# Hymba-style block on one core: the output projection moved into a stage of its own, as Strassen blocks per pair of token tiles

## What is computed

```python
h = rmsnorm(x, norm1_w);  proj = h @ w_in            # 1024 -> 2816
qa, ka, va, qb, fb, ib, gb = split(proj)
ya = sliding_window_attention(qa, ka, va, ...)       # 512 columns, 8 heads, window of 2 chunks of 64
yb = hgrn2(qb, fb, ib, gb, ...)                      # 512 columns, 4 heads, gated linear recurrence
x = x + concat(ya, yb) @ w_out                       # 1024 -> 1024: the output projection
h = rmsnorm(x, norm2_w);  gate, up = split(h @ w_gate_up)
x = x + (silu(gate) * up) @ w_down                   # d_ff = 2816
```

## Time and profile before

| | us |
|---|---|
| median of 3 runs | 2197.1 (2196.92 to 2197.79) |
| the profiled execution's own time | 2197.5 |
| its span, first to last instruction | 2195.7 |
| phase A, until the last matmul of WO3 | 894.85 |
| output projection in blocks 0 to 3, from its first matmul to the next block's | 51.86, 51.81, 51.85, 48.87 |

### The profile page before, as it was taken

The page is one execution under the profiler, slowest core; times in us unless marked ns, Lnnn a source line. Parts: engine busy times, 40 slices in busy tenths (PEclk is TensorE's granted clock), DMA queues, the critical chain, the costliest instruction groups (busy, mean ns, idle before and its releaser), DMA issues.

```text
span 2195.7 us, 30926 instructions
## 1 busy us (share of the span) xinstructions
PE 2139.9 (97%) x12376; PEld 1856.1 (85%) x12376; DVE 1337.5 (61%) x1967; ACT 904.7 (41%) x1575; POOL 132.6 (6%) x138
## 2 busy tenths in 40 slices
PE   7999999999999998799999999999999999999999
PEld 7889988998899888788888888888888888888887
DVE  4675367636753677567777667777777764444432
ACT  4774377437733762433323334333233332222221
POOL 2101110120012000100000000000000000000000
PEclk9999999999999999899999999999999999999999
DMA  3322232223223326634445335554444575645532
GB/s 138 136 78 91 102 136 78 97 97 139 75 97 105 136 82 237 229 117 141 156 152 187 101 115 187 177 191 140 164 155 146 181 253 175 214 166 179 186 132 91
DMA packets 156271, 316.22 MB, mean 144 GB/s; under 512 B 9504, under 2 KB 96800, under 8 KB 140128
## 3 DMA queue, kind: packets, MB, share of 16 engines
q1 hardware_dynamic: 144864, 265.74, 35.5%
q0 software_dynamic: 11264, 48.50, 6.1%
HBM read 230.85 MB, written 83.36 MB: 143 GB/s over the span
## 4 chain that ended last, share of the span: by engine, by line
PE 58%; DMA 0%; issue 0%; DVE 0%; POOLq 0%
PE b_bank_A L248 4%; PE b_bank_A L249 4%; PE b_bank_A L250 4%; PE b_bank_B L249 4%; PE b_bank_C L249 4%; PE b_bank_B L248 4%; PE b_bank_C L248 4%; PE b_bank_C L250 4%; PE b_bank_B L250 4%; PE b_hx_bank L1614 3%; PE b_hx_bank L1615 3%; PE b_hx_bank L1613 3%; PE b_bank_D L248 2%; PE b_bank_D L249 2%; PE b_bank_D L250 2%; PE b_hx_bank L1558 1%
## 5 line engine op out<-in xcount | busy, mean ns | idle before, releaser
L248 PE MATMUL a_pj<-a_w_hi,a_hT_hi 128*128 128x256 f32 x896 | 259.5, 290 | 1.7 <-issue 1.7
L249 PE MATMUL a_pj<-a_w_lo,a_hT_hi 128*128 128x256 f32 x896 | 253.6, 283 | 0.0
L250 PE MATMUL a_pj<-a_w_hi,a_hT_lo 128*128 128x256 f32 x896 | 253.6, 283 | 0.0
L1501 ACT ACTIVATE b_s_hi<-b_s_stage 128x1408 fp32r<-128x1408 f32 x56 | 77.4, 1382 | 300.1 <-PE b_hx_bank L1615 149.8
L924 DVE TENSOR_TENSOR a_w_lo<-a_w_stage,a_w_hi 128x2048 fp32r<-128x2048 f32 (+1 forms) x64 | 137.9, 2155 | 72.8 <-ACT a_w_hi L587 72.8
L248 PEld LDWEIGHTS a_pj<-a_w_hi,a_hT_hi 128*128 128x128 f32 x896 | 171.9, 192 | 6.7 <-issue 4.4
L249 PEld LDWEIGHTS a_pj<-a_w_lo,a_hT_hi 128*128 128x128 f32 x896 | 172.0, 192 | 0.0
L250 PEld LDWEIGHTS a_pj<-a_w_hi,a_hT_lo 128*128 128x128 f32 x896 | 171.8, 192 | 0.0
L248 PE MATMUL b_bank_A<-b_h_hi_B,b_w_hi 128*128 128x512 f32 x352 | 137.6, 391 | 0.0
L248 PE MATMUL b_bank_B<-b_h_hi_T,b_w_hi 128*128 128x512 f32 x352 | 137.3, 390 | 0.0
L250 PE MATMUL b_bank_A<-b_h_hi_B,b_w_lo 128*128 128x512 f32 x352 | 137.2, 390 | 0.0
(11 more groups left out here) (280 smaller groups left out, 5526.9 us busy)
## 6 DMA issues: line engine op xcount, KB each, us to landing
a_w_stage<-w_whole SPq DMA_DIRECT2D x56, 1024.0 KB, 4.8
b_gu_stage<-w_gu SPq DMA_DIRECT2D x44, 1024.0 KB, 5.1
b_s_stage<-a_sums SPq DMA_DIRECT2D x56, 704.0 KB, 4.2
a_sums<-b_a SPq DMA_DIRECT2D x88, 256.0 KB, 5.5
a_sums<-b_gate SPq DMA_DIRECT2D x66, 256.0 KB, 4.1
b_hx<-hc POOLq DMA_DIRECT2D x13, 1024.0 KB, 5.3
b_w_blocks<-w_dn SPq DMA_DIRECT2D x11, 1024.0 KB, 4.7
a_x_res<-x_pad POOLq DMA_DIRECT2D x16, 512.0 KB, 5.4
```

Source lines behind the costliest of these rows:

```text
L248: pe.matmul(out, stationary[0](k), moving[0](k), start=(k == 0 and not adds), stop=False, skip_group_check=adds)
L249: pe.matmul(out, stationary[0](k), moving[1](k), start=False, stop=False, skip_group_check=adds)
L250: last = pe.matmul(out, stationary[1](k), moving[0](k), start=False, stop=(k == ends), skip_group_check=adds)
L1501: act.activation(f.s_hi[n % 2][:], f.s_stage[n % 2][:], ACT.Copy).then_inc(f.s_hi_ready, 1)
```

## The change

The chunks WO0 to WO3 leave the blocks. The outputs of attention and recurrence are written to DRAM (`y_parts`) in full precision, without a split. In block 0, POOL works out the sums T1 to T4 of w_out's four blocks of 512 x 512 and they are stored (`wo_sums` in DRAM). Behind the last block stands a stage of its own. It takes token tiles in eight pairs (tile q of one block with tile q of the next): each pair is a 2 x 2 block product by Strassen's scheme in Winograd's form, seven products of 12 matmuls with 512 moving columns in place of eight. The seven right-hand operands (high and low) stay in SBUF, four of them prepared within block 3. The left-hand operands are loaded from `y_parts`; POOL makes the sums S1 to S4, ACT the high and DVE the low parts. DVE adds each product into the residual, which SP loads; ACT squares, SP stores x_mid, and for the pairs 0 to 3 DVE mixes straight from that tile (`scale`, `mix`) in place of the reload in block 3.

The core of the diff:

```diff
-NW = len(CHUNKS) + D // WC
+NW = len(CHUNKS)
...
-    after("I23", 3, ("hb", 3),)
-    after("G23", 0, ("ds", 2, 0), ("ds", 2, 1), ("hc", 3), ("n1a",))
-    after("G23", 1, ("o", 2), ("on1", 2), ("kt", 3), ("n1b", 0), ("n1b", 1))
-    after("G23", 2, ("on2", 2), ("ds", 3, 0), ("ds", 3, 1), ("att", 3))
-    after("G23", 3, ("on3", 2), ("o", 3), ("on1", 3), ("yt", 2), ("n1b", 2), ("on2", 3), ("on3", 3), ("n1b", 3))
-    after("Q23", 1, ("mix", 0, 0))
...
-    after("WO0", 0, ("xT", 0))
...
+    after("I23", 3, ("hb", 3), ("n1a",))
+    after("G23", 0, ("ds", 2, 0), ("ds", 2, 1), ("hc", 3), ("n1b", 0), ("n1b", 1))
+    after("G23", 1, ("o", 2), ("on1", 2), ("kt", 3), ("n1b", 2), ("n1b", 3))
+    after("G23", 2, ("on2", 2), ("ds", 3, 0), ("ds", 3, 1), ("att", 3), ("xT", 0), ("xT", 1))
+    after("G23", 3, ("on3", 2), ("xT", 2), ("xT", 3), ("o", 3), ("on1", 3), ("yt", 2), ("xT", 4), ("xT", 5), ("xT", 6), ("xT", 7))
...
+LAST_HEAD = {("KV", 0): (("on2", HG - 1), ("on3", HG - 1)), ("KV", 1): (("yt", HG - 1),)}
+PRODUCTS_OUT = ("P1", "P5", "P6", "P3", "P7", "P2", "P4")
...
+    at[("KV", 0)] = at.get(("KV", 0), ()) + (("wo_load", 0),)
+    at[("KV", 1)] = at.get(("KV", 1), ()) + (("wo_sums", 0),)
+    at[("KV", 3)] = (("wo_store", 0), ("wo_load", 1))
+    at[("QA0", 0)] = (("wo_sums", 1),)
+    at[("QA0", 2)] = (("wo_store", 1), ("wo_load", 2))
+    at[("QA0", 3)] = (("wo_sums", 2),)
...
+            ("G23", 0): tuple((part, 0, j) for j in (1, 2) for part in ("a_hi", "a_lo")),
+            ("G23", 1): (("t_hi", 3), ("t_lo", 3)),
+            ("G23", 2): tuple((part, 0, j) for j in (3, 4) for part in ("a_hi", "a_lo")),
+            ("G23", 3): tuple((part, 0, j) for j in (5, 6) for part in ("a_hi", "a_lo")) + (
+                ("x_load", 0, 0), ("t_load", 4), ("x_load", 0, 1), ("t_load", 5), ("t_load", 6))}
...
+    after(0, 0, ("on2", HG - 1), ("on3", HG - 1))
+    after(0, 1, ("yt", HG - 1), ("t_hi", 4), ("t_lo", 4), ("a_load", 1))
+    after(0, 2, ("n2w_load",), ("t_hi", 5), ("t_lo", 5))
+    after(0, 3, ("a_sums", 1))
+    after(0, 4, ("t_hi", 6), ("t_lo", 6))
+    for p in range(1, OUT_PAIRS):
+        after(p, 0, *([("a_load", p + 1)] if p + 1 < OUT_PAIRS else []))
+        if p - 1 < MIXED_PAIRS:
+            after(p, 1, ("scale", p - 1))
+            after(p, 2, ("mix", p - 1), ("mix_store", p - 1))
+        if p + 1 < OUT_PAIRS:
+            after(p, 3, ("a_sums", p + 1))
+    for p in range(OUT_PAIRS):
+        if p + 1 < OUT_PAIRS:
+            after(p, 4, *operands(p + 1, 0, 1))
+            after(p, 5, ("x_load", p + 1, 0), *operands(p + 1, 2, 3, 4))
+            after(p, 6, ("x_load", p + 1, 1), *operands(p + 1, 5, 6))
+        after(p, 6, ("mid", p))
...
+        def later_x(b, k):
+
+            if k == KT // 2:
+                for late in (KT - 2, KT - 1):
+                    at = TR_USES.index((b - 1, ("xT", late)))
+                    bank_read(at)
+                    transpose_x(b - 1, late, at, tr[at % 2])
...
+                elif kind == "out":
+                    p, j = step[1:]
+                    name, adds = PRODUCTS_OUT[j], PRODUCTS_OUT[j] in ("P6", "P7", "P3")
+                    pe.wait_ge(a_ready, NPO * p + j + 1)
+                    if p == 0:
+                        pe.wait_ge(t_ready, j + 1)
+                    if j >= 2:
+                        pe.wait_ge(c_added, sums_out(p, j - 1))
```

More of the change, by code:

```diff
@@ L58, in chunk_name @@
 def chunk_name(n):
[L59 removed]
+    return CHUNKS[n][0]
 def chunk_groups(n):
@@ new lines, in out_prepared @@
+def out_prepared():
+    return {("Q01", 0): (("t_load", 0),), ("Q01", 1): (("t_load", 1),),
+            ("I01", 1): (("t_hi", 0), ("t_lo", 0)), ("G01", 0): (("t_hi", 1), ("t_lo", 1)),
+            ("F23", 1): (("t_load", 2),), ("Q23", 1): (("t_hi", 2), ("t_lo", 2)),
+            ("I23", 0): (("a_load", 0),), ("I23", 2): (("a_sums", 0),), ("I23", 3): (("t_load", 3), ("a_hi", 0, 0), ("a_lo", 0, 0)),
+            ("G23", 0): tuple((part, 0, j) for j in (1, 2) for part in ("a_hi", "a_lo")),
[3 more added lines that the diff above has]
+                ("x_load", 0, 0), ("t_load", 4), ("x_load", 0, 1), ("t_load", 5), ("t_load", 6))}
@@ new lines, in out_steps, with after, operands @@
+def out_steps():
+    at = {}
+    def after(p, j, *steps):
+        at.setdefault((p, j), []).extend(steps)
+    def operands(p, *js):
+        return [(part, p, j) for j in js for part in ("a_hi", "a_lo")]
+    after(0, 0, ("on2", HG - 1), ("on3", HG - 1))
[16 more added lines that the diff above has]
+        after(p, 6, ("mid", p))
+    steps = []
+    for p in range(OUT_PAIRS):
+        for j in range(NPO):
+            steps.append(("out", p, j))
+            steps += at.pop((p, j), [])
+    assert not at, at
+    return steps
@@ new lines, in plan @@
+def plan():
+    steps = []
+    for b in range(NB):
+        extra = out_weight_sums({}) if b == 0 else out_prepared() if b == NB - 1 else {}
+        for step in STEPS:
+            if b == NB - 1 and of_next_block(step):
+                continue
+            steps.append((b, step))
+            if step[0] == "proj":
+                place = (chunk_name(step[1]), step[2])
+                if b > 0:
+                    steps += [(b - 1, late) for late in LAST_HEAD.get(place, ())]
+                steps += [(b, early) for early in extra.get(place, ())]
+    return steps + [(NB - 1, step) for step in out_steps()]
@@ L326, in build_phase_a @@
     carry = put("a_carry", [P, HG, P], F32)
+    y_at = mem.at
+    yA = [put(f"a_yA{s}", [P, HG, P], F32) for s in range(2)]
+    yH = [put(f"a_yH{s}", [P, TB], F32) for s in range(2)]
     y_nat = put("a_y_nat", [P, TT, P], F32)
@@ L972, in _ @@
         dve.tensor_scalar(one_less_lb[:], lb[:], -1.0, 1.0, ALU.mult, ALU.add)
-        for b in range(NB):
-            use = 0
-            for step in STEPS:
-                if left_out(step, b):
-                    continue
+        use = 0
+        for b, step in PLAN:
+            if True:
                 kind = step[0]
@@ L1832, in laid_out @@
         "w_whole": np.stack(whole),
+        "w_o": np.stack([rows.reshape(2, KT // 2, P, 2, 512)[k, :, :, half] for k, half in ((1, 1), (0, 1), (0, 0), (1, 0))], axis=2),
         "ident": np.eye(P, dtype=np.float32),
```

647 lines of the change are left out of this document (393 added, 254 removed).

## The result

| | before | after |
|---|---|---|
| median, us | 2197.27 (2196.92 to 2197.79, 4 runs) | 2229.56 (2227.94 to 2230.92, 4 runs) |
| span of the profiled execution | 2195.7 | 2227.5 |

The ratio is 1.0146, 95% interval 1.0134 to 1.0158. The forecast was 2175.3, in a range of 2153 to 2191: the sign was wrong, by 54 us. The part that was predicted to leave PE did leave it; waits in block 0, at the seams, in block 3 and in the new stage, and a lower clock behind most of them, more than made up for it.

The account below looks back on a forecast made before the run. PE, busy 97% of the span, was taken as the bound. Terms -41.5 - 1 + 14.4 - 3.7 + 2 + 3 + 6 - 1 = -21.8 us took the profiled 2197.5 to 2175.7, median 2175.3; range 2153 to 2191.

Parts of the forecast that it names:

- price of a pair, 19.05: Output projection stage: seven products of 12 matmuls take 19.05 us, as one phase B unit; eight pairs 152.4 us.
- block 0: First block: POOL's weight sums delay the powers of the norms behind them, so PE waits; +2 us.
- seams: Three passages between blocks: transposes of the next block wait for DVE's state chain and bank emptying; +14.4 us.
- block 3: Last block: the mixing stall goes, -8.8 us, but operand splits delay the state chain, +5.1; together -3.7 us.
- start of the stage: Beginning of the new output projection stage: 5 MB of loads issued after G23,3 arrive late; +3 us.
- within pairs 1 to 4: Mixing pairs: POOL's sums may hold up DVE, 11 us if so, 0 if not; half taken, +6 us.
- step to phase B: From the last pair to phase B: an earlier end of the stage against 4.5 MB loading at once; -1 us.
- PE's own -41.5: Output projection on PE: 193.9 us of work leaves, 152.4 us comes in; -41.5 us.
- the -1 of small waits: DVE beside PE's work: small waits removed as splits and low parts change; -1 us.
- Rival 2: Pairs 1 to 4: POOL and DVE lock each other, 11 to 16 us, 2180 to 2186; chance 0.20 shared with rival 4.
- Rival 4: Seams: the granted clock falls, 1 to 2 us each, +5, giving 2181; chance 0.20 shared with rival 2.
- Rival 3: Stage pairs: operands come late, each of 7 pairs waits 4 to 5 us, +32, 2198 to 2210; chance 0.09.

Follow-up runs that it names:

- the version without stalls: Changed kernel with block 0, mixture-split, block 3 and seam edits plus three small placement edits, without earlier phase B loads: 2178.8 us, ratio 0.9914.
- where block 3 had been mended: Changed kernel with block 3's preparations each placed where nothing waits behind them, pair 1's operand load not moved: 2214.6 us, ratio 1.0068.
- the three small edits: Pair 1's operands loaded one product earlier, fourth weight tile converted behind G23's last product, two of pair 0's operands within pair 0; not timed alone.
- the last two runs: Changed kernel with all edits together, with and then without the earlier loads of phase B: 2174.7 us (0.9894) and 2178.8 us (0.9914).

## Why the prediction was wrong

By its own steps, with what each term came to in the changed kernel and in the version without stalls (the last of the runs):

| term | predicted | changed | without stalls |
|---|---|---|---|
| price of a pair, 19.05 | 0 | +3.3 | +3.3 |
| block 0 | +2 | +10.8 | +1.2 |
| seams | +14.4 | +20.6 | +14.2 |
| block 3 | -3.7 | +16.6 | -8.5 |
| start of the stage | +3 | +4.1 | +5.5 |
| within pairs 1 to 4 | +6 | +17.7 | +5.9 |
| step to phase B | -1 | +1.2 | +0.9 |

PE's own -41.5 and the -1 of small waits stand beside these terms in the prediction; what was measured of the small waits is in the other rows. In the last column block 0 and block 3 are taken to and from the transposes of k. The seams' 14.2 is 521.83 us for three blocks, less the 653.03 of before without the 145.4 that left; it holds 1.9 us that POOL's moved sums cost in the rest of block 0. Where exactly the last product ends makes some 0.5 us in the sums.

- **PE's work: right, slightly mis-sized.** A pair without mixing takes 19.46 to 19.49 us, not 19.05: 0.4 x 8 = 3.3. The share that the prediction gave to the better price per column, some 11 us, was a slip: its own 169.7 less 152.4 is 17.3. The sum did not use it.
- **Block 3 is the step that failed most.** "That puts the chain 3.6 us later ... together PE reaches the stage 5.1 us late" came out as a wait of 9.72 us with its half clock, and block 3 as 16.6 us longer than before. I followed the state chain of G23,0 but not what came ahead: POOL's sums could only begin at 708.64, behind the split of G23, so the high part came at 714.35, with head 3's decay, its exponentials, a table load and then the next high parts strung behind it. And I had costed `t_lo` 0 and 1 at nothing beside the softmax, where they made waits of 2.87 and 3.63. The last run, with each step in a harmless place, shows that the work itself costs block 3 next to nothing: it then takes 8.5 us less than before, as "-8.8" said, while the stage's start, where two operands went, costs 1.4 more.
- **Within the pairs: mechanism named, wrong half taken.** The prediction gave 11 us "if DVE were held up alike" and took 6. It was held up: 17.7 us, in the pairs 2 to 4 2.6 to 2.7 us of waiting each plus the clock's 1.7. "The trace shows POOL held up, never DVE" is a right reading of the trace before, in which DVE's two-input operations run beside a power unhindered (53.16 above). But a power of 10 columns is not a sum of 512, and the trace before had no such sum; I let the one stand for the other. Rival 2's mechanism is the true one; its size lacked the clock.
- **The granted clock: dismissed wrongly.** Rival 4 was argued away with "the seams' waits are in pieces of under 3 us". Waits of 2.28 to 2.44 us at the seams and of 2.6 to 2.7 in the pairs 2 to 4 brought the lower clock. This went through the whole sum: all waits were entered at their own length. Between the changed kernel and the last run PE's busy time fell by 17.7 us with the same work.
- **Seams: the mechanism right, the size too small.** The wait at xT 0 was foretold at 2.5 us and is 2.28 to 2.44; 14.4 was said, 20.6 came, and with that wait gone 12.3. Of the 8.2 between them 3.6 are this wait (2.44, 2.28 and 2.29 less three times 1.13), the rest goes with the clock.
- **Block 0: a load's landing.** +2 was said, +10.8 came. Mechanism as said, but the third load landed at 54.61 and not at 48.5, so the powers started 13 us late and not 6, and the wait of 8.34 us also drew 10.2 us at half clock.
- **Rival 3**, late operands, did not decide: only pair 1 waited for them, 0.89 us in the changed kernel, and 3.72 where block 3 had been mended.
- **Stage start and step** lay within their bounds (+4.1 for +3, +1.2 for -1); in the version without stalls pair 0 is the slowest stretch left (24.9 us).

The stall-free version lands at 2178.8 where I had forecast 2175.3. So the forecast was one of a schedule that nothing falls out of. In this schedule POOL stood before a load in block 0, and DVE several times in block 3 before a high part that was not ready, each time with PE's next need queued behind. That it lands within 3.5 us is in part luck: its terms miss by +3.3 (price of a pair), +2.5 (stage's start), +1.9 (step) and -4.8 (block 3), which in part cancel. What stays open: how the 12.3 us of the seams divide between ACT and DVE, and what the three small edits that only the last two runs have are worth each; these were not run alone.

## What to carry to other kernels

When steps are added to an engine that works in order, ask of each not how long it takes but when its input is ready and what stands behind it; the conversion of 2.29 us whose input came 5.88 us late cost PE a wait of 2.87 and a half clock behind it. Price a wait with the clock that follows it: here one of 2.67 us cost 4.4. POOL's sums and DVE's operations with two inputs in SBUF were here to be costed as if on one engine; and where a trace shows only one of two engines as the loser, look whether the other ever met the same kind of operation.

## What the runs showed of the hardware

- PE's clock falls within a wait or up to 1.8 us behind its end. In these traces, behind the kernel's start, waits of 0.8 to 1.7 us brought no fall; most of those of 1.9 to 3.7 brought 3.4 us at 1.2 GHz and some 6.8, while one of 3.18, two of 2.87 and three of 2.16 brought none; waits of 4.3 to 5.9 brought 6.8 to 10.2, and those of 7.7 to 12.8 brought 6.8 to 17.
- The times of the kernels with many such waits spread more: 3.0 to 7.6 us in four runs each, with 2214.05 to 2221.65 in one of them, the fastest at a mean granted clock of 0.988, the others at 0.985. The kernel before spread over 1.3 to 3.8 us in seven runs, the two last versions over 1.4 and 2.3 in four.
- POOL's 128 x 512 float32 sum takes 1.29 us by itself, 1.5 to 2.1 beside the mixture, 3.15 beside DVE's subtraction of 2048 columns (2.29 us by itself, 3.22 there). DVE's scan over two SBUF inputs is stretched too, 1.22 to 2.31. A power of 10 columns on POOL and a product of 640 columns on DVE that starts behind it leave each other alone (1.96 and 0.83 us).
